# The last up-projection piece of the experts, loaded by sixteen transfers of 8 rows each

## The reference, cut to what matters

```python
def expert_block(args):
    xblk, e = args
    hid = jax.nn.silu(xblk @ w_gate[e]) * (xblk @ w_up[e])
    return hid @ w_down[e]
...
y = jnp.zeros((n_tok + 1, d), ht.dtype).at[tok_buf].add(out * w_buf[:, None])
x = x + hier_moe(rms_norm(x, ln_moe_g[l]), ...)
```

## Time and profile before

| | us |
|---|---|
| median of 3 runs | 1459.82 (1459.47 to 1463.4) |
| the profiled execution, own time | 1460.15 |
| its span | 1458.0 |
| TensorE's mean granted clock | 0.914 |
| PE busy | 1149.9 (79%) |
| DMA queue q1 (SP's), share of 16 engines | 79.8% |
| moved | 479.06 MB, mean 329 GB/s |

### The profile page before, as it was taken

One profiled execution on the slowest core, in us unless ns is written; L12 is line 12 of the kernel. 1 busy time (PEld: TensorE's weight loads), 2 busy tenths in 40 slices (PEclk: granted clock), 3 DMA queues, 4 the chain that ended last, 5 costly groups with the idle time before them and its releaser, 6 DMA issues.

```text
span 1458.0 us, 19738 instructions
## 1 busy us (share of the span) xinstructions
PE 1149.9 (79%) x8515; PEld 590.7 (41%) x8515; DVE 611.1 (42%) x1281; ACT 209.8 (14%) x458; POOL 15.2 (1%) x31
## 2 busy tenths in 40 slices
PE   6999999999999899867664877667765776577666
PEld 5885564665884553322221322222222222222222
DVE  4889999678453443312221323112221222122312
ACT  4211012273012311100000100000000000000000
POOL 4000000000000000000000000000000000000000
PEclk9999999999999999988887988878888899888988
DMA  9443352612437679999999999999999999999996
GB/s 295 148 146 136 137 202 109 227 55 87 174 125 258 243 294 423 425 427 428 425 430 426 427 426 428 427 427 428 427 426 429 427 427 428 426 429 425 428 427 261
DMA packets 73526, 479.06 MB, mean 329 GB/s; under 512 B 14885, under 2 KB 21413, under 8 KB 45152
## 3 DMA queue, kind: packets, MB, share of 16 engines
q1 hardware_dynamic: 72176, 477.45, 79.8%
q0 software_dynamic: 864, 0.25, 0.1%
q10 hardware_dynamic: 400, 0.10, 0.0%
HBM read 475.67 MB, written 2.11 MB: 328 GB/s over the span
## 4 chain that ended last, share of the span: by engine, by line
PE 47%; DMA 44%; DVE 3%; ACT 3%; issue 1%; SPq 0%; DVEq 0%; ACTq 0%
DMA late_ring<-in_moe_w_up_dram 23%; DMA ring<-in_moe_w_up_dram 17%; PE bank L652 10%; PE bank L1163 8%; PE bank L673 6%; PE bank L943 5%; PE bank L1123 3%; DMA late_ring<-in_moe_w_down_dram 3%; PE bank L1210 2%; PE bank L1197 2%; PE bank L1053 2%; PE bank L934 2%; PE bank L636 1%; PE bank L1019 1%; ACT hT L1357 1%
## 5 line engine op out<-in xcount | busy, mean ns | idle before, releaser
L1163 PE MATMUL bank<-ring,x_gathered 128*32 128x256 f32 x2432 | 289.9, 433 | 126.4 <-DMA late_ring<-in_moe_w_up_dram 86.4
L2429 DVE TENSOR_TENSOR tokens_out<-tokens_out,bank 128x512 f32<-128x512 f32 x240 | 148.9, 682 | 440.0 <-PE bank L1210 440.0
L1163 PE MATMUL bank<-late_ring,x_gathered 128*32 128x256 f32 x1664 | 235.0, 433 | 84.8 <-DMA ring<-in_moe_w_up_dram 84.7
L1163 PEld LDWEIGHTS bank<-ring,x_gathered 128*32 128x32 f32 x2432 | 130.6, 122 | 240.3 <-issue 208.4
L1163 PEld LDWEIGHTS bank<-late_ring,x_gathered 128*32 128x32 f32 x1664 | 103.0, 122 | 156.5 <-issue 136.7
L652 PE MATMUL bank<-ring,hT 128*128 128x512 f32 (+2 forms) x416 | 156.3, 536 | 3.4 <-ACT hT L1357 2.6
L1123 PE MATMUL bank<-x_tok,select 128*32 128x512 f32 x512 | 115.8, 1032 | 6.4 <-DVE select L2330 3.2
L652 PEld LDWEIGHTS bank<-ring,hT 128*128 128x128 f32 x416 | 78.6, 190 | 78.5 <-issue 67.0
L2385 DVE TENSOR_TENSOR x_gathered<-bank,gain_cols 128x512 f32<-128x512 f32 x32 | 22.1, 692 | 185.7 <-PE bank L1148 185.7
L1654 ACT ACTIVATE x_slots<-bank 128x512 f32<-128x512 f32 x32 | 19.1, 597 | 475.9 <-PE bank L1123 475.9
L1210 PE MATMUL bank<-y_slots,weight_slots 32*128 32x512 f32 x496 | 82.1, 736 | 6.7 <-DVE tokens_out L2429 5.2
(11 more groups left out here) (431 smaller groups left out, 1106.5 us busy)
## 6 DMA issues: line engine op xcount, KB each, us to landing
ring<-in_moe_w_gate_dram SPq DMA_DIRECT2D x36, 2048.0 KB, 38.3
ring<-in_moe_w_up_dram SPq DMA_DIRECT2D x35, 2048.0 KB, 42.9
ring<-in_moe_w_down_dram SPq DMA_DIRECT2D x35, 2048.0 KB, 38.1
late_ring<-in_moe_w_up_dram SPq DMA_DIRECT2D x25, 2048.0 KB, 42.8
late_ring<-in_moe_w_gate_dram SPq DMA_DIRECT2D x24, 2048.0 KB, 38.4
late_ring<-in_moe_w_down_dram SPq DMA_DIRECT2D x23, 2048.0 KB, 38.5
ring<-in_w_in_dram SPq DMA_DIRECT2D x20, 1024.0 KB, 9.3
ring<-in_w_out_dram SPq DMA_DIRECT2D x16, 1024.0 KB, 5.6
```

What stands on the lines that cost most here:

```text
L1163: mm = pe.matmul(gu_bank[SLOTS * c:SLOTS * c + SLOTS, 0:256], XGT[:, at, k % 4, k // 4, :], pieces[c // 2][:, a:a + 256], start=k == 0, st ...
L2429: ins = v.tensor_tensor(y, x, mix[c][:, :], ALU.add)
```

## The change

The piece q = 3 of expert 31 is loaded by sixteen transfers in place of one. Each takes 8 of the 128 partitions, every fourth one of a block of 32. The bytes, their place and the length of a row (16 KB) are the same. Each of the sixteen adds 16 to the semaphore, so that the count which PE waits for is larger by 15 times 16.

```diff
+        BY_ROWS = MAIN_PIECES - 3
...
+                elif g == BY_ROWS:
+                    for r in range(0, P, 32):
+                        for a in range(r, r + 4):
+                            sp.dma_start(shape4(moe_slot(i)[a:r + 32:4, :], q),
+                                         moe_source(j, q)[a:r + 32:4, :, :]).then_inc(main_in[i], 16)
                 else:
                     sp.dma_start(shape4(moe_slot(i), q), moe_source(j, q)).then_inc(main_in[i], 16)
...
-                    return main_in[slot], 16 * uses + (16 if g >= MAIN_PIECES - 2 else 0)
+                    return main_in[slot], 16 * (uses + (15 if g == BY_ROWS else g >= MAIN_PIECES - 2))
```

## The result

The changed kernel takes 1478.24 us in the median of 4 runs (1475.18 to 1478.8), beside 1461.61 in 4 runs of the kernel before: a ratio of 1.011, with an interval of 1.0095 to 1.0126, some 16 us. The sign is that of the prediction; the size is three times that of its sum (+5.5), and the time lies 9.6 us above its range. The profiled execution took 1477.7 with a span of 1475.9, 17.9 more than before. In the kernels of the experiments they differ again; the names tell what is meant.

The account below looks back on a forecast made before the run. Arriving up-projection weight pieces were taken to bound the kernel, the changed piece being the last link. Terms 4.92 + 0.1 + 0.5 gave +5.5 us, 1465.3 us as a median; main case +3.1 to +8.5, whole range 1459.4 to 1468.6.

Parts of the forecast that it names:

- Eight rows to eight engines: In the sixteen new transfers: each eight-row transfer uses eight engines, one for each row.
- Always the same eight: In the sixteen new transfers: all share one engine set, each engine carrying 256 KB instead of 128 KB.
- The set of eight is the lagging half: At the changed piece: its engines are the half some 9 to 10 us behind, giving a slowdown; chance 0.72.
- (a): At the changed piece's landing: the slowest engine takes twice 4.92 us, adding 4.92 us, or 3.1 at least.
- clue of one late share at 56 us: In the small eight-row write from ScalarE: one engine served it 0.6 to 1.2 us late, taken as fetching instructions.
- (e): At the partitions other engines usually write: two engines meeting there cost 0 to 2.5 us, taken as 0.
- (b): On each engine of the set: fifteen more completions add 0.1 us, between 0 and 0.6.
- (c): On PE after a longer idle before the changed piece: a lower clock adds 0.5 us, bounds 0 to 1.
- (d): On SP: sixteen issues instead of one take 5.3 to 6.9 us, all hidden, adding 0.
- SP held: Rival at SP's issues: each of sixteen held 2.88 us, down pieces land late, 1470 us and more; chance 0.04.
- leading half: Rival at the changed piece: engines that are ahead carry it, landing 4.9 us earlier, 1456.6 us; chance 0.14.
- even spread: Rival at the changed piece: every engine keeps 128 KB, only added completions remain, 1460 us; chance 0.10.

Follow-up runs that it names:

- lower kernel: All sixteen transfers of the change, but the eight carrying rows 64 to 127 write into the token tensor's lower 64 partitions: 1466.31 us beside 1460.8 before.
- kernel with an eighth of the share: Against the lower kernel, the eight transfers of rows 64 to 127 carry only the first eighth of each row: 1463.41 us beside 1461.79 before.
- upper kernel: Against the lower kernel, the eight transfers of rows 64 to 127 write into the token tensor's upper 64 partitions: 1476.12 us beside 1460.8 before.

## Why the prediction was right in sign and wrong in size

What bounds the kernel: right. Every delay of the changed piece came out at the end.

Eight rows to eight engines: right, by the count of packets. Always the same eight: it fits, since the lower kernel was 4.92 us later from wait to wait, as a double share at 26.6 GB/s an engine gives; no row shows an engine's number.

The set of eight is the lagging half: wrong as it stands, though (a) held. With it, the share would have been at one half from about 1430, as the prediction said, and in the lower kernel, where no engine disturbs another, until about 1450. The DMA view of the lower kernel, 1422 to 1446 us, shows otherwise:

```profile
DMA  9999999898999999978999999898964222111111
GB/s 437 437 423 437 437 416 382 362 382 355 416 403 355 389 416 382 396 287 355 362 369 416 376 430 437 362 369 348 375 280 184 96 82 82 75 68 75 55 55 48
```

The share is nearly full until 1440, and then 82 to 75 GB/s are three engines at 26. So only about three or four of the slowest engines are in the set, others of it had been ahead, and the lagging engines outside it were relieved of the piece. The landing is that of the slowest, so those few suffice for the whole of (a). The clue of one late share at 56 us said that much and no more; "if the fetching engines are one half of the sixteen, it is that half" went beyond it. It may have mattered for (e) too, since engines of the set that lead and partners that lag, and the other way round, would meet for longer; no run separates this.

The sign was said to hang on that reading. It did not. Two 64-row transfers (+13 us) and eight 16-row ones (+11.5) spread the piece evenly over sixteen engines (their queue has 72192 and 72288 packets, so 16 completions for each transfer), with no double share, and were slower all the same. So the sign is right in part by luck: of some 16 us only about 5 came by the way that the prediction describes, and the rest by a cost that it had put at 0.

(a) +4.92: right within about 1 us. The lower kernel has 4.92 from wait to wait; by the kernel with an eighth of the share, seven eighths of it were worth 3.2, so a whole one 3.7.

(b) +0.1 for completions, bound 0.6: open. The kernel with an eighth of the share kept about 1 us that the share does not explain.

(c) +0.5 for the clock, bounds 0 to 1: small in two kernels, not in a third. In the change, after 18.68 us of idling the clock granted was 0.50 (1.2 GHz) again; the 32 matmuls took 3.64 us and the combine 1.94, 5.6 together with no gap against 4.5 before, and the tail from the wait to the end is 1.2 longer. In the lower kernel, after 7.17 us, the tail is 23.40 against 22.56, +0.8, near the upper bound. But in the upper kernel, after 17.79 us and also at 0.50, it is 22.36, 0.2 less than before: the 32 matmuls took 3.23 us and the combine 1.07, for the clock rose again between the two (1.00, 2.4 GHz, from 1455.5 to 1456.7; in the lower kernel's combine, 1445.1 to 1446.8, it was 0.68). So the length of the idle alone does not give this term.

(d) 0 for SP: right as far as the runs show, though the issues were taken too short. The sixteen issues took 18.71 us, not 5.3 to 6.9, and pushed the last down piece's issue to 1437.95; PE asked for it at 1464.42 (1446.73 before), and the kernel cut by columns, with 15.09 us of issues, cost nothing. PE did not wait at its last products, and the rival "SP held" is out as the cause of the 16 us. The 1 us under (b) could be the issues'.

(e) 0 for two engines at the same partitions, bound 2.5: this is the step that failed. The measured price is 9.8 us, the gap between the upper and the lower kernel. It failed in two ways. First, I took the value at the lower end although no row spoke for it, arguing that "the leading ones have by then little left". Second, the bound counted one side of the meeting only, and half of a share of it. Both engines that meet are slowed: the eight foreign rows of an engine take 1.22 us instead of 0.62 each, +4.9, and the engines that own these groups have their rows slowed as well, which made the piece ahead 5.5 us late (6.2 between the lower and the upper kernel) and, if it is on the slowest engines, their start on the changed one with it. 4.9 and 5.5 make 10.4, near the 9.8. With the order turned round the sum of the waits stayed the same, as this count has it. The price is measured; this count of how it comes about is my reading, for no row tells which engine met which.

The Trainium skill's page on "SBUF — State Buffer" was at hand and had the map, though no price for two engines at one port. I read from its section on the port swizzle only that the eight engines of one transfer don't meet each other, which is true, and not whom the rows 64 to 127 belong to. By its map (bit 6 chooses the other port of a pair) eight engines that serve all 128 rows must enter the ports of the other eight.

The sum with (e) at its measured value: 4.92 + 0.1 + 0.5 + 9.8 = +15.3, against 16.6 (the gap of the medians) or 16.1 (1.1%). It is no test of its own, since (a) and (e) are read from the lower and the upper kernel, and these two steps make up the upper one's +15.3.

The rivals: the leading half would have been faster, and the even spread unchanged; both are out by the 4.92. The direction's chance of 0.68 was fair; the range was not, since the one cost that nothing in the trace priced was given a bound by argument. The bounds of the steps also add up to more than the range that was written down: 4.92 + 0.6 + 1 + 2.5 = +9.0, not +8.5. The measured time lies far above either.

No run here beat the kernel before. Of the ways to cut the piece, the two that reach all groups evenly, by columns and by even and odd rows, were level with it. One that takes load off the lagging engines was not tried.

## What to carry to other kernels

When a load is cut along the partitions, ask for each part which groups of partitions it reaches and who else writes them at that time: an eight-row transfer put its load on eight engines here, and rows of the other engines' half of SBUF delayed transfers that were not cut at all. Cutting by columns, or by even and odd rows, cost nothing; cutting at partition 64 cost as much as 13 us on a 2 MB piece. In these traces a DMA share near 1 at half of the usual GB/s was engines in each other's way, and a share of one half at half of the rate was engines out of work; look at both numbers. And a cost that no row prices needs a bound that counts everyone who meets there, before any argument that few do.

## What the runs showed of the hardware that was not expected

- Where engines write each other's partitions, a busy one moves 13.4 instead of 26.4 GB/s, and for 10 us this was the mean over all sixteen (210 GB/s at a share of 0.98, no more than eight engines move), for a single 2 MB piece that eight of them carry.
- The disturbance reaches pieces issued before it: 44.0 to 49.5 us from issue to landing.
- Eight rows next to each other are hardly worse than eight that lie four apart (+19 against +16 us), where four times the packet time was expected.
- SP's issues of partial transfers took 1.2 us each (18.71 for 16) and 3.8 each (15.09 for 4) with some nine pieces outstanding, where whole pieces just before took 0.33 and 0.43; the 15.09 us cost nothing.
